# Row buffers handed out one by one in the expert stage: slots taken from the weight buffers piece by piece, last raw chunks loaded by halves, query halves and expert groups in another order

## The reference

```python
def peer_ffn(h, w_query, sub_keys, u_emb, v_emb):          # in chunks of 128 tokens
    q = (hc @ w_query).reshape(B, T_CHUNK, PEER_HEADS, 2, PEER_DKEY // 2)    # 8 heads, 2 x 128
    s = jnp.einsum('bthpd,hpnd->bthpn', q, sub_keys)
    s_top, i_top = lax.top_k(s, 16)                         # per head and half: 16 of 128 keys
    cand = s_top[..., 0, :, None] + s_top[..., 1, None, :]  # 256 pairs
    g_s, pos = lax.top_k(cand, 16)                          # the 16 best pairs: expert numbers e_idx
    g = jax.nn.softmax(g_s, axis=-1)
    u = u_emb[e_idx]
    act = gelu(jnp.einsum('btd,bthkd->bthk', hc, u))
    return jnp.einsum('bthk,bthkd->btd', g * act, v_emb[e_idx])
```

## Time and profile before

| what | us |
|---|---|
| median of 3 runs (1940.65 to 1941.59) | 1940.66 |
| the profiled execution | 1942.27 |
| its span | 1941.0 |
| TensorE busy in the span | 1755.3 (90%) |
| VectorE busy | 1285.5 (66%) |
| ScalarE busy | 801.1 (41%) |
| Pool busy | 651.1 (34%) |
| queue of the gathers and of adaW (software dynamic) | 301.52 MB |

### The profile page before, as it was taken

The page is one execution under the profiler, slowest core; times in us unless marked ns, Lnnn a source line. Parts: engine busy times, 40 slices in busy tenths (PEclk is TensorE's granted clock), DMA queues, the critical chain, the costliest instruction groups (busy, mean ns, idle before and its releaser), DMA issues.

```text
span 1941.0 us, 23001 instructions
## 1 busy us (share of the span) xinstructions
PE 1755.3 (90%) x8086; PEld 1288.6 (66%) x8086; DVE 1285.5 (66%) x2238; ACT 801.1 (41%) x1447; POOL 651.1 (34%) x602
## 2 busy tenths in 40 slices
PE   7999999999999999999999899799887787877877
PEld 5887898887888888988878888665433332333322
DVE  4566866566566656676565785688678788865554
ACT  5444435544354435675443556533221232311112
POOL 4443551044204442034441012123443343333330
PEclk9999999999999999999999999899899899998999
DMA  8999985799989999958997975399999999999995
GB/s 265 325 364 392 319 299 207 261 332 364 362 294 336 356 366 331 322 206 297 349 363 274 276 251 166 133 362 359 417 420 421 419 421 420 419 420 421 420 421 234
DMA packets 247066, 649.43 MB, mean 335 GB/s; under 512 B 14866, under 2 KB 156483, under 8 KB 214212
## 3 DMA queue, kind: packets, MB, share of 16 engines
q1 hardware_dynamic: 200004, 345.63, 52.2%
q0 software_dynamic: 46304, 301.52, 38.9%
q10 hardware_dynamic: 672, 1.18, 0.2%
HBM read 643.04 MB, written 139.48 MB: 403 GB/s over the span
## 4 chain that ended last, share of the span: by engine, by line
PE 55%; DMA 26%; DVE 12%; ACT 4%; issue 2%; SPq 0%; POOL 0%; DVEq 0%; ACTq 0%
DMA late_uv<-uv_rows,M 11%; PE P L1323 9%; DMA early_uv<-uv_rows,M 7%; PE PX L831 6%; PE PX L833 6%; PE PX L832 6%; PE P L737 4%; PE P L739 4%; PE P L738 4%; DMA WR<-in_ffn_w_up 4%; DVE WL L1912 3%; DMA WR<-in_ffn_w_down 3%; PE P L686 2%; PE P L687 2%; PE P L688 2%
## 5 line engine op out<-in xcount | busy, mean ns | idle before, releaser
L1912 DVE TENSOR_TENSOR WL<-WR,WH 128x1024 fp32r<-128x1024 f32 (+1 forms) x246 | 329.1, 1379 | 196.0 <-ACT WH L1381 195.8
L1381 ACT ACTIVATE WH<-WR 128x1024 fp32r<-128x1024 f32 (+1 forms) x272 | 270.9, 1044 | 319.1 <-PE P L739 116.5
L1323 PE MATMUL P<-early_uv,M 128*128 128x512 f32 x576 | 279.3, 642 | 66.7 <-ACT M L1829 66.7
L831 PE MATMUL PX<-WH,hTh 128*128 128x512 f32 x704 | 280.2, 398 | 6.9 <-DVE WL L1920 4.4
L833 PE MATMUL PX<-WH,hTl 128*128 128x512 f32 x704 | 275.3, 391 | 0.0
L832 PE MATMUL PX<-WL,hTh 128*128 128x512 f32 x704 | 274.6, 390 | 0.0
L1927 DVE TENSOR_TENSOR WL<-WR,WH 128x1024 fp32r<-128x1024 f32 x128 | 177.8, 1430 | 136.6 <-ACT WH L1390 136.6
L1323 PE MATMUL P<-late_uv,M 128*128 128x512 f32 x432 | 213.7, 652 | 58.7 <-ACT M L1829 58.7
L1323 PEld LDWEIGHTS P<-early_uv,M 128*128 128x128 f32 x576 | 115.4, 206 | 225.0 <-issue 141.1
L671 POOL DMA_INDIRECT early_uv<-uv_rows,M x144 | 139.0, 965 | 284.1 <-PE P L1323 182.7
L2568 DVE CUSTOM_DVE_ANT_0 early_uv<-early_uv,PX 128x1024 f32<-128x1024 f32 x144 | 171.8, 1219 | 78.1 <-DMA early_uv<-uv_rows,M 77.4
(11 more groups left out here) (391 smaller groups left out, 3182.6 us busy)
## 6 DMA issues: line engine op xcount, KB each, us to landing
WR<-in_ffn_w_up SPq DMA_DIRECT2D x88, 1024.0 KB, 10.0
WR<-in_ffn_w_down SPq DMA_DIRECT2D x44, 1024.0 KB, 11.1
uv_rows<-in_peer_u SPq DMA_DIRECT2D x37, 1024.0 KB, 13.8
uv_rows<-in_peer_v SPq DMA_DIRECT2D x37, 1024.0 KB, 13.9
uv_rows<-in_peer_u SPq DMA_DIRECT2D x54, 512.0 KB, 10.1
uv_rows<-in_peer_v SPq DMA_DIRECT2D x54, 512.0 KB, 9.5
adaW<-in_w_ada POOLq DMA_DIRECT2D x48, 512.0 KB, 8.2
WR<-in_diff_w_in SPq DMA_DIRECT2D x14, 1024.0 KB, 13.3
```

The lines of the kernel that those rows point to most:

```text
L831: mm(o, xh, WH[:, u, w], start=(k == 0), stop=False)
L1323: last = mm(P[2 * t + q][:], diag[:, n % 2, i], rows_uv(n)[:, i, D + q * 512:D + q * 512 + 512], start=n % GROUPS == 0 and i == 0, stop=n ...
L1381: nc.scalar.activation(split_view(WH, U % 2, kind, part), raw(c % 2, kind, h, part), copy)\
L1912: tt(split_view(WL, U % 2, kind, part), raw(c % 2, kind, h, part), split_view(WH, U % 2, kind, part).bitcast(F32), ALU.subtract)\
```

## The change

The slot of every gather now comes from a list, `SLOT`, one entry a gather. From gather 48 on it is the old one (number modulo 16). Before that, most gathers go round the 8 early slots; gathers 16, 17 take slots 8 and 9, gathers 28 to 31 slots 8 to 11, gathers 40 to 47 slots 8 to 15. A gather into a late slot that nobody has used yet waits for the weight buffer under it: raw buffer 0 or 1 read for the last time, or the last half of that parity used. The wait for all halves at group 10 is gone.

The third and fourth raw chunk are loaded half by half: the first half as soon as the half that lay there has been split, the second likewise, and not before the first has landed, so that ScalarE can wait for a half.

`second_tile` replaces the full half 0: 24 matmuls with the second tile's h as weights, a copy and two transposes on TensorE with two copies on ScalarE, as in `first_tile`.

The order: VectorE does group 0's products ahead of the split of half 3; TensorE runs half 3 before groups 0 and 1; the later groups move by one place; the gates of the second call are made just ahead of group 4.

```diff
+    REGULAR = 12 * NG
+    TAKEN_OVER = {16: 8, 17: 9, 28: 8, 29: 9, 30: 10, 31: 11, **{40 + i: 8 + i for i in range(8)}}
+    def slots():
+        first = 0
+        for at in range(2 * GROUPS * NG):
+            if at >= REGULAR:
+                yield at % 16
+            elif at in TAKEN_OVER:
+                yield TAKEN_OVER[at]
+            else:
+                yield first % 8
+                first += 1
+    SLOT = list(slots())
+    def user_before(n, i):
+        at = n * NG + i
+        return max((m for m in range(at) if SLOT[m] == SLOT[at]), default=None)
...
-    V_AFTER = {2: (0,), 3: (1,), 4: (2, 3), 5: (4, 5), 6: (6, 7), 7: (8,)}
-    U_AFTER = {1: (0,), 2: (1,), 3: (2, 3), 4: (4, 5), 5: (6, 7), 6: (8,), 7: (9,)}
+    V_AFTER = {3: (0, 1), 4: (2,), 5: (3, 4), 6: (5, 6), 7: (7, 8)}
+    U_AFTER = {2: (1,), 3: (2,), 4: (3, 4), 5: (5, 6), 6: (7, 8), 7: (9,)}
...
         def load(c):
             kind, n, parts, special = chunks[c]
-            if c >= 2:
+            by_half = c >= phases["wq"]["C"] + 2
+            if c >= 2 and not by_half:
                 sp.wait_ge(S["lo_ready"], last_half[c - 2] + 1)
             for q, src in enumerate(parts):
+                if by_half:
+                    sp.wait_ge(S["lo_ready"], last_half[c - 2] + q)
+                    if q:
+                        sp.wait_ge(raw_landed[c % 2], slot_loads[c] - 16)
                 sp.dma_start(raw_dst_of(c % 2, kind, q), src).then_inc(raw_landed[c % 2], 16)
...
+        def last_user(what, parity):
+            return max(u for u, (c, h) in enumerate(half_of) if (u if what == "half" else c) % 2 == parity)
         def gather(n):
             call = ALL_CALLS.index((n // GROUPS, n % GROUPS * NG // 16))
             pool.wait_ge(S["index_ready"], call + 1)
-            if n == EARLY:
-                pool.wait_ge(S["half_used"], len(half_of))
             for i in range(NG):
                 at = n * NG + i
-                if user_before(n) is not None:
-                    pool.wait_ge(S["v_used"], NG * user_before(n) + i + 1)
-                pool.indirect_dma_start(rows_uv(n)[:, i, :], None, uv_rows,
+                if user_before(n, i) is not None:
+                    pool.wait_ge(S["v_used"], user_before(n, i) + 1)
+                elif SLOT[at] >= 12:
+                    pool.wait_ge(S["half_used"], last_user("half", SLOT[at] % 2) + 1)
+                elif SLOT[at] >= 8:
+                    pool.wait_ge(S["lo_ready"], last_user("raw", SLOT[at] // 2 % 2) + 1)
+                pool.indirect_dma_start(row_uv(n, i), None, uv_rows,
...
+        def second_tile():
+            U, E = p["U"], p["E"]
+            o = P[4 + E % 2]
+            pe.wait_ge(S["bank_free"], E - 1)
+            for k in range(KT):
+                if k % 2 == 0:
+                    pe.wait_ge(S["hl_ready"], 36 + k // 2 + 1)
+                w = slice(k * 256, k * 256 + 256)
+                xh, xl = hTh[:, k, 128:256], hTl[:, k, 128:256]
+                mm(o[:, 0:256], xh, WH[:, U % 2, w], start=(k == 0), stop=False)
+                mm(o[:, 0:256], xh, WL[:, U % 2, w], start=False, stop=False)
+                last = mm(o[:, 0:256], xl, WH[:, U % 2, w], start=False, stop=(k == KT - 1))
+            last.then_inc(S["half_used"], 1)
+            rows_of_h(1)
+            pe.wait_ge(S["qtok_ready"], 2)
+            for b in range(2):
+                last = nc.tensor.transpose(o[:, 256 + b * 128:256 + b * 128 + 128], qtok[:, b * 128:b * 128 + 128], ident[:])
+            last.then_inc(S["qtok_turned"], 1)
+        second_tile()
-        for j in range(8):
+        for j in range(1, 8):
...
-            act.wait_ge(raw_landed[c % 2], slot_loads[c])
+            act.wait_ge(raw_landed[c % 2], slot_loads[c] - (16 if U >= WQ_U + 4 and h == 0 else 0))
...
         tile_high(1)
+        act.wait_ge(S["half_used"], WQ_U + 1)
+        nc.scalar.activation(qtok, P[4 + WQ_E % 2][:, 0:256], copy).then_inc(S["qtok_ready"], 1)
+        act.wait_ge(S["qtok_turned"], 2)
+        nc.scalar.activation(pQ[:, 0, :, 128:256], P[4 + WQ_E % 2][:, 256:512].rearrange("p (a b) -> p a b", a=2), copy)\
+            .then_inc(S["bank_free"], 1)
...
         for j in range(8):
+            if j == 1:
+                gate_exps(0)
             split(p["U"] + j + 2)
             if j == 1:
-                gate_exps(0)
-            if j == 3:
-                gate_exps(1)
+                experts(0)
...
             for n in U_AFTER.get(j, ()):
+                if n == 4:
+                    gate_exps(1)
                 experts(n)
...
-                dve.wait_ge(S["half_used"], p["U"] + 1)
-                nc.vector.tensor_copy(pQ[:, 0, :, 128:256], P[4 + p["E"] % 2][:].rearrange("p (a b) -> p a b", a=2)[:, :, 128:256])\
-                    .then_inc(S["bank_free"], 1)
             else:
                 post_copy(p["U"] + j, p["E"] + j, pQ[:, j % 4])
-            split(p["U"] + j + 2)
             if j == 1:
                 dve.wait_ge(S["htok_tr"], 2)
                 gates(0)
-            if j == 3:
-                gates(1)
+                experts(0)
+            split(p["U"] + j + 2)
             for n in U_AFTER.get(j, ()):
+                if n == 4:
+                    gates(1)
                 experts(n)
                 sort_and_choose(n)
```

More of the change, by code:

```diff
@@ L97, in program, with row_uv, turn @@
     early_uv = sb("early_uv", [128, 2, NG, 2 * D])
[L99 to L109, removed]
+    REGULAR = 12 * NG
[11 more added lines that the diff above has]
+    SLOT = list(slots())
+    def row_uv(n, i):
+        slot = SLOT[n * NG + i]
+        return early_uv[:, slot // NG, slot % NG] if slot < 8 else late_uv[:, slot // NG - 2, slot % NG]
+    def turn(n, i):
+        at = n * NG + i
+        return SLOT[:at + 1].count(SLOT[at])
+    def user_before(n, i):
+        at = n * NG + i
+        return max((m for m in range(at) if SLOT[m] == SLOT[at]), default=None)
     PX = ctx.enter_context(nc.psum_tensor("PX", [128, 2, 1024], F32))
@@ L220, in program @@
     raw_landed = [sem("raw_landed0"), sem("raw_landed1")]
-    uv_landed = [[sem(f"uv_landed{g}{i}") for i in range(NG)] for g in range(4)]
+    uv_landed = [sem(f"uv_landed{slot}") for slot in range(16)]
     b_landed = [sem("b_landed0"), sem("b_landed1")]
@@ L1322, in experts @@
                 for q in range(2):
-                    last = mm(P[2 * t + q][:], diag[:, n % 2, i], rows_uv(n)[:, i, D + q * 512:D + q * 512 + 512],
+                    last = mm(P[2 * t + q][:], diag[:, n % 2, i], row_uv(n, i)[:, D + q * 512:D + q * 512 + 512],
                               start=n % GROUPS == 0 and i == 0, stop=n % GROUPS == GROUPS - 1 and i == NG - 1, skip_group_check=True)
                 last.then_inc(S["v_used"], 1)
-        for j in range(8):
+        def second_tile():
[18 more added lines that the diff above has]
+        for j in range(1, 8):
             U, E = p["U"] + j, p["E"] + j
[L1329 to L1332, removed]
+            cols_half(U, U % 2, E, E % 2, between=(lambda: subkey_scores(0)) if j == 1 else None)
             if j > 1:
@@ L1362, in _ @@
             for q in range(2):
-                mm(P[2 + q][:], diag[:, LAST % 2, i], rows_uv(LAST)[:, i, D + q * 512:D + q * 512 + 512], start=False, stop=i == NG - 1,
+                mm(P[2 + q][:], diag[:, LAST % 2, i], row_uv(LAST, i)[:, D + q * 512:D + q * 512 + 512], start=False, stop=i == NG - 1,
                    skip_group_check=True).then_inc(S["v_used" if q else "left_used"], 1)
@@ L2566, in experts @@
             for i in range(NG):
-                dve.wait_ge(uv_landed[ring(n)][i], r * 16 + 16 * turn(n))
-                last = nc.vector.tensor_tensor_reduce(out=u[:, i, 0:D], in0=u[:, i, 0:D], in1=HTOK[n // GROUPS], scale=1.0, scalar=0.0,
+                dve.wait_ge(uv_landed[SLOT[n * NG + i]], r * 16 + 16 * turn(n, i))
+                u = row_uv(n, i)[:, 0:D]
+                last = nc.vector.tensor_tensor_reduce(out=u, in0=u, in1=HTOK[n // GROUPS], scale=1.0, scalar=0.0,
                                                       op0=ALU.mult, op1=ALU.add, accum_out=dots[:, g, i:i + 1])
```

11 lines of the change are left out of this document (6 added, 5 removed).

## The result

The changed kernel takes 1932.35 us (median of 5 runs, 1928.82 to 1935.1), the kernel before 1941.59 on the same chip (5 runs, 1940.65 to 1944.81): 9.2 us less by the medians. The ratio is 0.995 with a 95% interval of 0.9933 to 0.9967, that is 6.4 to 13.0 us. The forecast was 1929.5, with 11.1 us gained.

A forecast was written before the change was run, and what follows sets the result against it. The gather stream's start was taken to bound the kernel: gather 8's landing at 1285.9, plus 3.0 for a load and 150.7 at full pace, puts gather 67 at 1439.6, 11.1 us earlier; hence 1929.5 us, forecast 1926 to 1934, range 1925.5 to 1937.

The forecast's parts named there:

- The bound: Gather stream: at 2.554 us a gather, the kernel ends a fixed time after the stream gets going.
- Second tile: Start of the wq stage: 24 matmuls instead of 48, priced at 5.1 us on the slow clock; half 1 starts 2.7 us earlier.
- Order: Halves and groups on TensorE: groups 0 and 1 from 1277.7, gather 8 issued at 1280.5, 1.2 us earlier.
- Buffers: Late slots in the wq stage: freed early enough for every gather, least slack 4 to 5 us, so holes close.
- The holes: Gaps in the gather stream behind gather 8, from waits for 8 buffers: 10.5 us lost before the change.
- gather 16 leaves at 1299: Pool's issue of gather 16, after the second choice and half 5's split: 1299 at latest, due at 1303.9.
- The slack: Time between a gather's possible issue and when the full stream needs it issued: least 4 to 5 us.
- Loads by halves: wq's third raw chunk: its first half moves before 1250, taking 1.05 MB, 3.0 us, out of the stage.
- TensorE and VectorE did not become the bound: Rival for the wq stage: slower-clock groups outlast the slack, 4.5 us come back, 1934, up to 1938; chance 17%.
- It does not do what it says: Rival: half 5's split well after 1304 holds gather 16; only 3.0 + 1.2 us remain, 1936.5, up to 1941; 9%.
- The loads did not starve: Rival: wq loads beside gathers land too late for half 7 and hold up slots; 1956 in its example; chance 4%.
- the prediction's limit, 1325: Time when half 7's split is due; its last raw load landing after about this holds up slots 10, 11, 13, 15.

The follow-up runs named there:

- doubled halves: Changed kernel with TensorE running half 4's matmuls twice, then halves 4 and 5 twice: 1933.51 us (ratio to before 0.9949) and 1938.05 us (0.9981).
- the run with group 1 ahead of the split: Changed kernel with chunks loaded whole and group 1's products ahead of half 4's split on VectorE and ScalarE: 1935.47 us, ratio to before 0.9964.
- group 0 first: Changed kernel with TensorE's group 0 right behind half 2, ahead of half 3: 1928.05 us, ratio to before 0.9932.
- the second run: The kernel with TensorE's group 0 ahead of half 3, run again beside the changed kernel on one chip: 1927.55 us, ratio to before 0.9933.

## Why the prediction was right, and where its terms were not

**The bound.** Right. The pace (40.87 for 16 gathers) and the time behind gather 67 (490.3) are those of before, so the gain is the earlier landing of gather 67. Forecast was a stretch of 1439.6 - 1250.13 = 189.5; it is 188.1. From gather 0's issue to gather 8's landing it had 35.8 and got 35.5, from there to gather 67 it had 153.7 and got 152.6: the sum is near in both parts, and not by two errors that cancel.

**Second tile.** It takes 4.6 us and not 5.1, and half 1 starts 5.6 after the tile's start and not 6.7, 1.1 better. The granted clock of that window is 0.74, a mixture of the two levels, where it was 0.50 before, after an idle time that is practically the same (6.07 against 6.08): the rows shrink from 0.41 to 0.28 us at 1253.2. The price from the slow window was near the upper end of what came: over the profiles of the kernels with this tile it took 4.3 to 5.3. That it was 4.6 here is luck of the clock.

**Order.** Groups 0 and 1 start 26.7 us after gather 0; forecast was 27.6 (1277.7 - 1250.13). Gather 8 leaves after 29.7, forecast 30.4. That part of the second tile's gain is spent on half 3 is what two kernels show: the tile alone brings gather 8 to 28.5, and the changed kernel with the old order does the same. It is 1.3 of 3.1 us, though, less than half, where the prediction wrote "mostly".

**Buffers.** The holes close as forecast: 410 GB/s or more in every window of 10 us behind 1290. The bound "gather 16 leaves at 1299" was 8 us too late, since choice and split come earlier than assumed: 1291.3. The slack was 4 to 5; doubled halves put it at 3.3 to 4.2. In the rows of the changed kernel it is least at gather 48, where the prediction had 6.6 to spare: that gather lands 8.2 us after its issue, 2.8 above the least of 5.4, and gather 26 lands 8.7 after. VectorE's wait for the gates of the second call, which was to cost nothing inside that slack, is in the waits of the changed kernel (engine, what it waits for: us in total, times, longest), between 1255 and 1380, with Pool's wait for TensorE:

```profile
POOL early_uv L697 <- PE P L1349: 36.4, 21, 7.4
...
DVE small L2215 <- ACT M L1866: 2.9, 1, 2.9
```

Pool's was 51.5 us in 26 waits before; its waits ahead of late slots, 5.6 in 2 before, are 9.8 in 4. Behind 1290 they come ahead of slots that the stream doesn't need yet: the rate stays full.

**Loads by halves: the mis-sized term.** The prediction counted them as bytes: 1.05 MB at 348 GB/s, "3.0 us, out of the stage". With whole loads the stretch is 6.0 longer, and the run with group 1 ahead of the split shows that none of it is bandwidth. The step that failed is the one that asked what the load takes from the gathers and not who waits for it: chunk 2's first half is half 4's raw data, its split stands in front of group 1's products on VectorE, and in this order of groups a load that lands at 1280.7 makes that split wait. The sum came out well all the same, because it took half 4's split as on time, which the halves make true. Where the term did enter, the 3.0 us for the load behind gather 8, it was a little large: gather 8 lands at 1278.83 + 5.7 = 1284.5, gather 67 at 1437.2, and 59 gathers at 2.554 are 150.7, so 2.0 us are lost behind gather 8, with what is left of the holes.

**The rivals.** TensorE and VectorE did not become the bound: groups 0 and 1 ran at the full clock, 13.90 us for both, and the wait of 4.14 ahead of them is gone. The doubled halves show that this rival stood some 4 us off. "It does not do what it says" needed gather 16 late; the kernel with the old slots is that case, and it shows 5.8 us of gain left where the rival's sum had 4.2. Where the other 1.6 come from was not run; the loads, worth more than the 3.0 in that sum, may hold it.

The loads did not starve. DMA issues of the changed kernel (queue, count, KB, us to landing): chunk 2's first half in the empty stretch, then chunk 3's two halves beside gathers:

```profile
WR<-in_peer_wq SPq DMA_DIRECT2D x1, 1024.0 KB, 5.4
...
WR<-in_peer_wq SPq DMA_DIRECT2D x1, 1024.0 KB, 20.4
...
WR<-in_peer_wq SPq DMA_DIRECT2D x1, 1024.0 KB, 22.7
```

The Trainium skill, "DMA: Bandwidth & Descriptors", section "Queues, rings and completion order", lets each engine take its queues in turn, packet by packet. The trace agrees in kind that a load beside gathers is served slowly (20.4 and 22.7 against 5.4), as before (24.7 and 6.8). Beside fuller gathers it is slower still: with group 0 first the same two loads took 29.2 and 26.3, and 29.2 and 25.3 in the second run, beyond 24.7, the longest that the prediction had a row for. The last of them landed 66.9 us after gather 0's issue; the prediction's limit, 1325, is 74.9 after it.

**The numbers.** The stretch came out 1.4 us better than forecast, the median 2.9 us worse (1932.35 against 1929.5). Of the 2.9, 0.9 is the base: the kernel before stood at 1940.66 in three runs and at 1941.59 in five. That leaves a gain of 9.2 where 11.1 was forecast, inside the interval of 6.4 to 13.0. The profile is of the fastest of the five runs, and its stretch has the whole gain; where the slower ones lose is not shown. Over the profiles the start of gather 0 scatters by some 7 us. What sets that start was not tested.

## What to carry to other kernels

Before pricing a load in a busy stage by its bytes, ask who waits for the last of them: the same MB cost 6.0 us with a group of products queued behind its split, and nothing once the group stood in front, since the stream left room for its bytes. Where the stream leaves no room the bytes seem to count too: with group 0 first, some 3 us of the lead went while the last load ran beside full gathers.

When a stream has one full pace, measure every edit by the stretch from its first issue to a late landing. Here that repeats to 0.2 and 1.3 us, where the whole times of the changed kernel scatter by 6.

And a gain at the head of a stream is kept only as far as what comes behind it allows. The second tile's 3.1 us met old buffers, and 1.5 were left; the 6.1 of group 0 first met the last load, and 2.2 were left, 1.2 in the second run.

## What the runs showed of the hardware

Pool takes 0.94 us to issue a gather, but up to 1.87 in some rows. Six of the 48 gathers between 1245 and 1375 in the changed kernel take over 1.05 us, and five of these begin while a split runs on VectorE, an operation with two inputs in SBUF (timelines of Pool and VectorE). A pair in which the gather begins inside the split, then one in which it begins ahead of it:

```profile
1325.16 1.87 POOL L697 DMA_INDIRECT early_uv<-uv_rows,M  x1 [4.86 <-PE P L1349]
```

```profile
1325.01 2.35 DVE L1963 TENSOR_TENSOR WL<-WR,WH 128x1024 fp32r<-128x1024 f32 x2
```

```profile
1257.34 0.94 POOL L697 DMA_INDIRECT early_uv<-uv_rows,M  x1 [0.31 <-issue]
```

```profile
1257.66 2.36 DVE L1963 TENSOR_TENSOR WL<-WR,WH 128x1024 fp32r<-128x1024 f32 x2 [2.79 <-ACT WH L1425]
```

A split is two instructions, one behind the other. Of the eleven gathers that overlap with one, the five that begin in its first half are longer, and each ends 0.32 to 0.33 us before the split does, however long it had to wait (1.12 to 1.87 us in all). Two begin ahead of the split and four in its last 0.02 us; these six take 0.94. In the kernel before, two gathers that begin in the second half of a split end 0.81 us behind it. So a gather that begins beside one of the two instructions looks as if it first waited for that one's end and then took its 0.94. The Trainium skill, "SBUF — State Buffer", section "Who interferes with whom", has a VectorE instruction with two SBUF inputs contend with a GpSimd instruction that reads SBUF; the rows fit that in kind, and put it at 0.9 us an issue at most here. No run here takes the split away, so the cause is not shown; at 0.9 us inside Pool's slack it costs this kernel nothing that can be seen.
